# Second layer, four steps: DVE norms the queries ahead of the sums with the bias instead of behind them

## What is computed

```python
def swa_layer(x, g_norm, w_in, g_q, sinks, w_out, k_band, v_band, bias, mask):
    proj = rmsnorm(x, g_norm) @ w_in
    q, gate = jnp.split(proj, [SWA_Q_WIDTH], axis=-1)
    q = rmsnorm(q.reshape(b, nb, BLOCK, SWA_KV_HEADS, SWA_GROUP, SWA_HEAD_DIM), g_q)
    scores = jnp.einsum('bnqkgd,bnjkd->bnkgqj', q, k_band).astype(jnp.float32)
    scores = scores * (SWA_HEAD_DIM ** -0.5) + bias[None, None]
    scores = jnp.where(mask[None, :, None, None], scores, -jnp.inf)
    m = jnp.maximum(jnp.max(scores, axis=-1, keepdims=True), sink)
    p = jnp.exp(scores - m)
    p = p / (jnp.sum(p, axis=-1, keepdims=True) + jnp.exp(sink - m))
    o = jnp.einsum('bnkgqj,bnjkd->bnqkgd', p.astype(v_band.dtype), v_band)
    o = o.reshape(b, s, SWA_Q_WIDTH) * jax.nn.silu(gate)
    return x + o @ w_out
```

## Time and profile before

| | |
|---|---|
| median of 3 runs | 2305.13 us (2304.97 to 2305.74) |
| profiled execution | 2303.87 us, its span 2302.1 us |
| PE busy | 2237.8 us, 97% of the span |
| PE weight loads busy | 1787.4 us, 78% |
| DVE, ACT, POOL busy | 1115.7, 874.5, 212.1 us (48%, 38%, 9%) |
| mean granted TensorE clock | 0.995 of full speed |

### The profile page before, as it was taken

One profiled execution on the slowest core, in us unless ns is written; L12 is line 12 of the kernel. 1 busy time (PEld: TensorE's weight loads), 2 busy tenths in 40 slices (PEclk: granted clock), 3 DMA queues, 4 the chain that ended last, 5 costly groups with the idle time before them and its releaser, 6 DMA issues. The chain is left out here.

```text
span 2302.1 us, 32368 instructions
## 1 busy us (share of the span) xinstructions
PE 2237.8 (97%) x11746; PEld 1787.4 (78%) x11746; DVE 1115.7 (48%) x3121; ACT 874.5 (38%) x2277; POOL 212.1 (9%) x313
## 2 busy tenths in 40 slices
PE   7999999999999998999999799999999999999998
PEld 6888888888888887777777677777777776888876
DVE  6264264254363124454554336666765766533342
ACT  4241241341352113545553234544544545532232
POOL 1000000000000001121110000010110100110023
PEclk9999999999999999999999999999999999999999
DMA  4111111111146213011134510111011102523322
GB/s 158 57 60 53 55 46 50 57 46 62 46 142 233 73 64 119 10 53 51 51 115 136 172 42 22 63 45 43 26 45 63 46 23 65 175 73 95 101 101 92
DMA packets 125013, 174.65 MB, mean 76 GB/s; under 512 B 7417, under 2 KB 73017, under 8 KB 123329
## 3 DMA queue, kind: packets, MB, share of 16 engines
q1 hardware_dynamic: 119072, 157.46, 20.7%
q10 hardware_dynamic: 5792, 15.24, 1.8%
HBM read 143.27 MB, written 29.42 MB: 75 GB/s over the span
## 5 line engine op out<-in xcount | busy, mean ns | idle before, releaser
L91 PE MATMUL heads_p_ps<-ret_w_second_hi_sb,ret_hT_hi_sb 128*128 128x512 f32 x384 | 150.5, 392 | 1.0 <-DVE ret_w_second_lo_sb L638 0.9
L91 PE MATMUL heads_p_ps<-ret_w_second_lo_sb,ret_hT_hi_sb 128*128 128x512 f32 x384 | 149.5, 389 | 0.0
L91 PE MATMUL heads_p_ps<-ret_w_second_hi_sb,ret_hT_lo_sb 128*128 128x512 f32 x384 | 149.4, 389 | 0.0
L91 PE MATMUL att_proj_ps<-br_w_second_hi_sb,br_hT_hi_sb 128*128 128x512 f32 x320 | 135.9, 425 | 0.0
L91 PE MATMUL att_proj_ps<-br_w_second_hi_sb,br_hT_lo_sb 128*128 128x512 f32 x320 | 125.4, 392 | 0.0
L91 PE MATMUL att_proj_ps<-br_w_second_lo_sb,br_hT_hi_sb 128*128 128x512 f32 x320 | 125.4, 392 | 0.0
L2441 ACT ACTIVATE br_x_sb<-br_x_sb,att_max_neg_sb 128x256 f32<-128x256 f32 (+7 forms) x128 | 97.8, 767 | 20.8 <-DVE att_max_neg_sb L2672 20.6
L91 PEld LDWEIGHTS heads_p_ps<-ret_w_second_hi_sb,ret_hT_hi_sb 128*128 128x128 f32 x384 | 72.1, 188 | 18.1 <-issue 2.8
L91 PEld LDWEIGHTS heads_p_ps<-ret_w_second_lo_sb,ret_hT_hi_sb 128*128 128x128 f32 x384 | 72.1, 188 | 15.1
L91 PEld LDWEIGHTS heads_p_ps<-ret_w_second_hi_sb,ret_hT_lo_sb 128*128 128x128 f32 x384 | 72.1, 188 | 14.6
L409 POOL TENSOR_TENSOR heads_o_rstd_sb<-heads_o_ms_sb,heads_minus_half_sb 128x1 f32<-128x1 f32 x32 | 17.6, 551 | 634.7 <-ACT heads_o_ms_sb L625 634.7
(11 more groups left out here) (563 smaller groups left out, 6323.4 us busy)
## 6 DMA issues: line engine op xcount, KB each, us to landing
early_w_kv_sb<-a_w_blocks SPq DMA_DIRECT2D x26, 1024.0 KB, 5.2
all_w_block_sb<-w_turns SPq DMA_DIRECT2D x12, 2048.0 KB, 9.4
br_y_raw_sb<-branch_yT_dram SPq DMA_DIRECT2D x32, 512.0 KB, 4.2
ret_o_dram<-early_x_rows_sb ACTq DMA_DIRECT2D x32, 256.0 KB, 2.4
all_w_block_sb<-swa_turns SPq DMA_DIRECT2D x4, 2048.0 KB, 9.0
heads_o_rows_sb<-ret_o_dram ACTq DMA_DIRECT2D x6, 1024.0 KB, 5.3
x_dram<-early_x_rows_sb SPq DMA_DIRECT2D x12, 512.0 KB, 2.8
all_w_block_sb<-a_w_blocks SPq DMA_DIRECT2D x2, 2048.0 KB, 9.4
```

What stands on the lines that cost most here:

```text
L91: mm = pe.matmul(out, rows[a], w[b], start=(k == 0 and a + b == 0), stop=(k == KT - 1 and b == 1))
```

## The change

In the steps in which `early_probs` is true, `norm_queries(n-1)` is issued right behind `copy_probs(n-3)` and ahead of `bias_max(n-2)`; in all others nothing changes. No instruction is added or removed, on DVE or elsewhere.

```diff
@@ -1719,9 +1719,10 @@
                 early_probs = t == 0
                 if early_probs:
                     copy_probs(n - 3)
+                    norm_queries(n - 1)
                 if 2 <= n < ITEMS + 2:
                     bias_max(n - 2)
-                if 2 <= n <= ITEMS:
+                if 2 <= n <= ITEMS and not early_probs:
                     norm_queries(n - 1)
                 if 3 <= n < ITEMS + 3 and not early_probs:
                     copy_probs(n - 3)
```

## The result

The changed kernel took 2308.37 us (median of 20 runs, 2304.85 to 2310.36) against 2305.49 us before (20 runs beside them, 2301.61 to 2306.85). The ratio is 1.0013, with a 95% interval of 1.0007 to 1.0019: 3.0 us slower, 1.6 to 4.4. The forecast was 2308.7 us and 3.6 us. The profiled execution has a span of 2306.0 us.

What follows compares the result with a forecast made beforehand. At four weight changes PE's scores were taken to wait on DVE's sums, ACT's exponentials and query copy. Four delays of 0.89 us gave 3.56 over the profiled 2303.87, plus 1.26 for the median: 2308.7 us, range 2305.7 to 2310.7.

Steps and rivals of the forecast that it cites:

- The binding chain: Second layer's weight changes: scores wait on DVE's sums, max_neg, ACT's exponentials and query copy; the norm's earlier start gains 0 us.
- The wait for POOL: DVE, moved norm at the four steps: waits 0.55 us for POOL's factor, delaying the sums.
- rival D: POOL's factor is there in time, leaving only the norm's own time: 1.4 us slower, 2306.5 us; chance 0.08.
- The norm's own time: DVE, four steps: the norm ahead of the sums delays them 0.34 us, start to start, not its busy 0.42.
- Sum: Four weight changes at 0.89 us each: 3.56 us slower, 2308.7 us.
- Nothing takes it up afterwards: Behind the four steps nothing absorbs the delay; the 5.08 us idle at the third layer's start shifts as a whole.
- Rival A: The delays as summed at the four weight changes: 2308.7 us, 3.6 us slower; chance 0.65.
- C: PE's waits for the norm at the query transposes are what counts: 2.66 us faster, 2302.5 us; chance 0.07.
- Rival B: TensorE's clock falls at step 32 after 2.30 us idle, costing 1.7 us more: 5.3 us slower, 2310.4 us; chance 0.15.

Runs made afterwards that it cites:

- e2: Against the kernel before: at the four weight changes the norm stands between DVE's second and third sum; ratio 1.0009, steps 1.31 us over before.
- e4: The changed kernel, with ACT copying the queries ahead of the exponentials at the four weight changes; ratio 0.9995, steps 3.72 us less than before.
- e1: Against the kernel before: DVE's order kept, only the wait for POOL's factor put ahead of the sums; ratio 1.0011, steps 2.26 us over before.
- e7: The changed kernel run once more, unedited, beside others on one chip; ratio 1.0015, 3.5 us over before.
- e5: Against the changed kernel: the norm ahead of the sums in all 31 steps that have one, not only four; ratio 1.0026, 6.0 us over before.
- e10: e4's kernel, with ACT's high part of the output tile moved ahead of the exponentials in step 32; ratio 0.9980, 4.6 us less than before.
- e3: The kernel before, with ACT copying the queries ahead of the exponentials at the four weight changes; ratio 1.0002, steps 0.97 us less than before.
- e6: The changed kernel, with three more multiplications into scratch memory ahead of the norm at the four steps; ratio 1.0045, 10.4 us over before.

## Why the prediction was right

- **The binding chain** (sums, `max_neg`, exponentials, copy of the queries, scores): right. e2 got the norm early without the wait and lost 0.33 us a step; e4 took the chain apart and the same move shortened the steps by 2.75 us (2.17 with step 33).
- **The wait for POOL**, which no row of before showed, was put at 0.55 us from the end of POOL's span and the 0.03 us of the earlier trace rows. e1 measured 0.55. The bound from below (rival D, factor usable earlier) is out.
- **The norm's own time**: 0.34 us by the distance of two starts and not the 0.42 us of its busy time. e2 measured 0.33 to 0.34. The Trainium skill (VectorE: DVE Perf Modes, "The DRAIN you can't avoid") states that the next operation waits until the pipe is empty, and in the same paragraph that one which isn't held starts earlier. The prediction gave 0.42 us as the price by the first of the two; the measured 0.34 us agrees with the second.
- **Sum**: 0.89 us a step forecast, 0.88 and 0.89 measured; 3.56 us against 3.53. In the runs it was 3.0 us (1.6 to 4.4) and, in e7, 3.5 us (1.2 to 5.5). The median of 2308.37 us lies nearer to the forecast of 2308.7 than the difference does, because the kernel before took 2305.49 us in the runs beside it and not the 2305.13 that the sum started from; that part is luck.
- **Nothing takes it up afterwards**: right within the spread. From the scores of step 33 to the third layer it takes 93.52 us before (1206.78 to 1300.30) and 93.85 with the change (1212.22 to 1306.07). The 0.33 us are the wait of PE for a row block near the end of the layer, 0.47 us in the one and 0.79 in the other. In the kernel before, DVE waited there for a DMA. The same wait is 1.18 us in e7, so it varies by more than this difference between profiles of one kernel.
- **Rival A against C**: the rule to start the dependency behind a gap sooner (the Trainium skill, Perfetto Trace Analysis, "Optimization Strategy"), applied to the larger wait in PE's list, would have given 2.7 us of gain; the steps lost 3.5 us. The larger wait was covered by the smaller one behind it.
- **Rival B's evidence was weaker than I put it.** I called an idle time of 1.83 us harmless because the clock stayed up around it. At the same place the clock fell in e5, with an idle time of 1.82 us, and in e10, with 1.84; in the other ten profiles, with 1.81 to 1.84 us, it stayed at 1.00. The stretches of e5 and of e10 around it:

```profile
1955.00:1962.00 7.00, 5.61 (x23) 3.39 (x23) 6.00 (x23) 3.26 (x10) 0.97 (x1) 0.76 0.00 0
...
1943.83:1950.83 7.00, 6.00 (x26) 3.61 (x27) 5.91 (x21) 3.26 (x10) 0.97 (x1) 0.76 0.00 0
```

  One profile that shows no fall behind an idle time doesn't make that length safe. The chance of 0.15 stood on that row, and the three idle times of 1.57 us were called harmless by it. The profiles of the change, e5 and e7 show no fall behind them or behind the 2.22 us, and nothing here excludes one.

## What to carry to other kernels

Two waits of one engine in a row are not two sums to be saved. Before a producer is moved forward for the first, follow back what ends the second: if it is a chain through the very instructions that the producer would be moved ahead of, the move costs its own time and the wait that it brings along. Compare also the whole step with an undisturbed one: the 10.01 us against 9.27 held both waits, and only the two moves together (e4, e10) took them out.

Where a chain has an engine that does nothing but wait, look for work of it that can be done in that time. In the changed kernel ACT waited 3.00 us for `max_neg` while the copy that PE needed stood behind four exponentials. The input of that work has to be there in time: in the kernel before the transposes came only at 982.78, behind the start of the exponentials, and the copy put first (e3) gained 0.97 us in the steps, where with the norm moved as well (e4) it was 3.72.

## What the runs showed of the hardware that I had not expected

- The clock's falls behind idle times of 1.8 to 2.4 us come in some executions and not in others. At one place of the third layer, whose code is the same in all, there was a fall in two of twelve profiles (e5 and e10, with idle times of 1.82 and 1.84 us). In e6 one came behind 2.39 us and none behind 2.40 and 2.39 us at two other changes of weights. The two falls inside e6's second layer cost 1.5 us each.
- The kernel's start differs between executions too: the first transposes of the second layer start at 873.42 us before and at 875.14 with the change, though nothing ahead of them differs. In the profile of the change the granted clock is 0.83 between 10 and 20 us, and it is 1.00 there in the kernel before: 10 x 0.17 = 1.7 us, which is the difference. But e2, e4 and e7 reach this place at 875.95 to 876.29 us with 1.00 shown from the start to 873 us, so the clock isn't the whole cause, and what else there is stays open. These are single profiles, and nothing was tested here by itself.
- POOL's power of a 128x4 tile takes 1.00 or 1.01 us each of the 32 times in every profile. A DVE instruction that waits for it starts 0.02 to 0.04 us after its shown end, so the span of this operation, of which I had been wary, could be used as it stands.
